# Two tiles of an output projection stand beside other heads of the attention in a two-layer SSD, retention and attention step

## The reference, cut to what matters

```python
u = h @ lp['w_in']
y_ssd, ssd_state = _ssd(...)        # 8 heads x 64
y_ret, ret_state = _retention(...)  # 4 heads x 64
y_mla, ckv, krope = _mla(...)       # 4 heads x 64, softmax attention
mix = jnp.concatenate([y_ssd, y_ret, y_mla], axis=-1)   # width 1024
x = x + g1 * (mix @ lp['w_out'])
h2 = _rmsnorm(x, lp['norm2_w']) * (1 + sc2) + sh2
a, gt = jnp.split(h2 @ lp['ffn_w1'], 2, axis=-1)
x = x + g2 * ((jax.nn.silu(a) * gt) @ lp['ffn_w2'])
```

## Time and profile before

| what | value |
|---|---|
| median of 3 runs | 1047.66 us (1045.16 to 1050.39) |
| the profiled execution's own time | 1046.3 us |
| its span | 1043.4 us |
| PE busy | 1017.8 us (98%) |
| DVE busy | 632.6 us (61%) |
| ACT busy | 439.5 us (42%) |
| mean granted clock of PE | 0.997 |

### The profile page before, as it was taken

How to read it: one execution, slowest core, us unless ns; L and a number is a source line. 1 busy time by engine, 2 the same in 40 slices (tenths; PEclk the granted TensorE clock), 3 DMA queues, 4 the chain that set the end, 5 groups by cost and what they waited for, 6 DMA issues and landing times.

```text
span 1043.4 us, 16435 instructions
## 1 busy us (share of the span) xinstructions
PE 1017.8 (98%) x6552; PEld 931.5 (89%) x6552; DVE 632.6 (61%) x1134; ACT 439.5 (42%) x684; POOL 105.3 (10%) x99
## 2 busy tenths in 40 slices
PE   7899999999999999999999999999999999999995
PEld 4698996779999989999999899667999999999995
DVE  6686868868555543534448786887765555444333
ACT  3256445456333332343334755735543333323221
POOL 0004323003000000000101233400300000000100
PEclk9999999999999999999999999999999999999998
DMA  9843245314333478333464224451243333723431
GB/s 382 335 165 128 82 161 202 130 64 149 139 132 128 161 291 325 112 113 114 136 244 161 92 84 150 165 216 41 90 153 121 121 121 121 278 89 111 132 117 60
DMA packets 30678, 159.56 MB, mean 153 GB/s; under 512 B 3424, under 2 KB 4384, under 8 KB 19872
## 3 DMA queue, kind: packets, MB, share of 16 engines
q1 hardware_dynamic: 28896, 146.75, 38.9%
q10 hardware_dynamic: 1728, 12.06, 2.8%
HBM read 156.27 MB, written 2.52 MB: 152 GB/s over the span
## 4 chain that ended last, share of the span: by engine, by line
PE 92%; DVE 4%; ACT 2%; ACTq 1%; issue 1%; DMA 1%; POOL 0%; DVEq 0%; POOLq 0%
PE ps L476 26%; PE ps L478 26%; PE ps L477 25%; PE ps L505 3%; DVE wlo L1356 1%; PE ps L803 1%; PE ps L720 1%; PE ps L922 1%; PE ps L747 1%; PE ps L572 1%; PE ps L901 1%; ACTq L1068 1%; PE ps L824 1%; ACT whi L1018 1%; DMA adas<-wada_dram 1%
## 5 line engine op out<-in xcount | busy, mean ns | idle before, releaser
L476 PE MATMUL ps<-h_hi,whi 128*128 128x386 f32 (+1 forms) x1120 | 384.7, 344 | 0.6 <-issue 0.5
L478 PE MATMUL ps<-h_hi,wlo 128*128 128x386 f32 (+1 forms) x1120 | 379.7, 339 | 0.0
L477 PE MATMUL ps<-h_lo,whi 128*128 128x386 f32 (+1 forms) x1120 | 378.7, 338 | 0.0
L1356 DVE TENSOR_TENSOR wlo<-stage,whi 128x2048 fp32r<-128x2048 f32 (+1 forms) x106 | 223.3, 2107 | 154.2 <-ACT whi L1018 154.2
L1018 ACT ACTIVATE whi<-stage 128x2048 fp32r<-128x2048 f32 (+1 forms) x106 | 185.9, 1754 | 229.1 <-PE ps L478 210.7
L476 PEld LDWEIGHTS ps<-h_hi,whi 128*128 128x128 f32 x1120 | 211.3, 189 | 9.5 <-issue 7.0
L477 PEld LDWEIGHTS ps<-h_lo,whi 128*128 128x128 f32 x1120 | 211.6, 189 | 0.3
L478 PEld LDWEIGHTS ps<-h_hi,wlo 128*128 128x128 f32 x1120 | 210.6, 188 | 0.0
L476 PE MATMUL ps<-hid_hi,whi 128*128 128x384 f32 x352 | 118.3, 336 | 0.0
L478 PE MATMUL ps<-hid_hi,wlo 128*128 128x384 f32 x352 | 118.3, 336 | 0.0
L477 PE MATMUL ps<-hid_lo,whi 128*128 128x384 f32 x352 | 118.3, 336 | 0.0
(11 more groups left out here) (295 smaller groups left out, 1131.1 us busy)
## 6 DMA issues: line engine op xcount, KB each, us to landing
stage<-wf_dram SPq DMA_DIRECT2D x44, 1024.0 KB, 4.8
adas<-wada_dram SPq DMA_DIRECT2D x80, 512.0 KB, 5.7
stage<-wf_dram SPq DMA_DIRECT2D x32, 704.0 KB, 4.1
stage<-win_dram SPq DMA_DIRECT2D x20, 1024.0 KB, 4.8
stage<-wout_dram SPq DMA_DIRECT2D x8, 1024.0 KB, 5.6
adaf<-wada_dram ACTq DMA_DIRECT2D x6, 1024.0 KB, 15.2
small<-small_dram SPq DMA_DIRECT2D x2, 1202.5 KB, 8.7
stage<-win_dram ACTq DMA_DIRECT2D x2, 1024.0 KB, 13.3
```

Of the source, the lines that this page charges most:

```text
L476: mm(out, ah, bh, start=(k == 0), stop=False)
L477: mm(out, ah, bl, start=False, stop=False)
L478: return mm(out, al, bh, start=False, stop=(k == n - 1))
L1356: tt(wlo[:, g % 2, 0:width], stage[:, g % 2, 0:width], whi[:, g % 2, 0:width].bitcast(F32), ALU.subtract)\
```

## The change

The list of the heads beside which the eight first-half tiles stand has 3 in place of 4 and 7 in place of 8. Tile 2 thus stands in step 3 of PE, tile 5 in step 7; DVE's residual of tile 2 stands in step 4, that of tile 5 in step 8 (ahead of the split of block 13 in that step). Tiles 0, 1, 3, 4, 6 and 7 keep their steps.

```diff
-BESIDE_HEADS = (1, 2, 4, 5, 6, 8, 9, 11)
+BESIDE_HEADS = (1, 2, 3, 5, 6, 7, 9, 11)
```

## The result

| | median of the runs | against before, ratio (95% interval) |
|---|---|---|
| before | 1047.01 us (12 runs) | |
| changed | 1053.65 us (12 runs, 1051.82 to 1058.15) | 1.0066 (1.0054 to 1.0077) |

The change makes the kernel slower by 6.6 us. The forecast was 4.2 us more (1051.9); the time lies in its range (1048.0 to 1055.5), but above the 0.5% within which the forecast saw its likeliest case.

What follows compares the result with a forecast made beforehand. PE was taken to bound the kernel (92% of the chain), taking turns with DVE in the attention. 2.41 - 0.33 = 2.08 us a layer, 4.2 for two, on 1047.66 gave 1051.9 us; range 1048.0 to 1055.5.

Steps and rivals of the forecast that it cites:

- likeliest case: Attention of both layers: the PE and DVE ping-pong is stretched ahead of the weight split, +2.0 to +5.2 us, 1051.9; chance 0.66.
- The replay of the order: Attention, PE and DVE timelines of layer 0 reworked with tiles 2 and 5 moved: 2.08 us a layer, 4.2 for two.
- transposes 8 start: PE, attention: delayed 2.41 us to 220.88, PE's wait of 0.67 there becoming about 2.7 us.
- the attention at full clock: Each layer's attention: 2.41 late at transpose 8 less 0.33 given back, 2.08 us longer.
- The residual of tile 2 now stands ahead of maximum 5: DVE, attention: this residual costs 0.55, so with the 0.90 of maximum 4, maximum 5 is late by 1.45 us.
- Behind a wait it takes 0.13 more: PE, transposes of head 4: 0.55 for three against 0.42 without a wait, putting scores of head 7 1.06 us late.
- Nothing in it absorbs a delay: DVE and ACT chain around the weight split, maximum 8 to transpose 8: the 2.41 us delay passes on whole.
- The give-back: Transpose 9 on PE: residual of tile 5 no longer behind normalisation 8, so a 0.28 wait and 0.05 restart go, 0.33.
- by the rows, it stayed at 1.00 through 2 us without a matmul, and the sum leaves it out: PE clock in the new wait of about 2.7 us: taken as staying at 2.4 GHz, no time added.
- rival (c): New wait before transpose 8: clock falls, work to tile 7's end takes twice as long, +4.8 a layer, +13.8, 1061.5; chance 0.03.
- or if the clock row shows under 1.00 in the attention: Sign against the prediction: granted clock in the attention was to read 1.00 in the changed profile.
- Rival (d): Not slower: tiles fill PE's waits before transposes 2 and 6, -1.2 us, 1046.5, if maximum 8 late leaves transpose 8 unaffected; chance 0.09.

Runs made afterwards that it cites:

- early split: ACT's high half of weight block 13 written in step 5, not 8: changed kernel 1047.21 us, 0.9997 of before; kernel before 1045.71 us, 0.9984.
- second run: The changed kernel itself timed and profiled once more, nothing further changed: 1054.85 us median, 1.0065 of before.
- the run with the filled wait: The changed kernel plus 14 matmuls of unused result per layer in PE's wait before the transposes of head 8: 1051.92 us, 1.0043 of before.

## Why the prediction was right, and where it fell short

**The replay of the order held.** Its times, and those of the changed kernel less the 0.15 of its later start:

| step of the prediction | forecast | measured |
|---|---|---|
| tile 2 starts | 197.95 | 197.95 |
| maximum 4 starts | 201.01 | 201.02 |
| transposes 4 start | 206.05 | 206.03 |
| scores of head 7 start | 209.18 | 209.09 |
| scores of head 8 start | 212.37 | 212.20 |
| transposes 8 start | 220.88 | 220.72 |
| PE's wait there | about 2.7 | 2.62 |
| the attention at full clock | +2.08 | +2.01 |

"The residual of tile 2 now stands ahead of maximum 5", at 0.55, was right: maximum 5 came at 204.71, and 203.27 + 1.45 is 204.72. "Behind a wait it takes 0.13 more" was half wrong: from transposes 4 to the products behind them it took 0.48 (206.18 to 206.66), so 0.06 more, and tile 5 follows its transposes by 0.24 (209.89 to 210.13) where 0.33 was taken; so everything from head 7 on came 0.1 to 0.2 earlier than forecast. "Nothing in it absorbs a delay" held: maximum 8 was 2.24 late and transposes 8 were 2.25 late. The runs with the early split show what could have absorbed some of it: there DVE doesn't wait for ACT in that chain, and 2.25 at maximum 8 become 1.24 at transposes 8. The give-back behind them can be read in layer 1, at full clock: transposes 8 were 2.25 late (26.88 us behind the first scores before, 29.13 now) and the attention 2.01 longer, so 0.24 was given back where the prediction had 2.41 and 0.33.

**The step that failed is the clock.** The prediction weighed it and then wrote "by the rows, it stayed at 1.00 through 2 us without a matmul, and the sum leaves it out", and gave rival (c) 0.03. By its own last sentence, "or if the clock row shows under 1.00 in the attention", it was wrong here, though the time came out in its range. But the earlier trace rows show one instance, at the end of the kernel, where no matmul follows: the last one ended at 1033.27 and the clock fell only in the stretch from 1036. That told little of a wait in the midst of the work. In the profiled executions with a wait of 2.6 us there are six such attentions, and the clock fell in five; in the four with the wait filled and the eight with no wait of transposes over 0.8 us it fell in none. The Trainium skill (TensorE: Matmul & The Clock Gate, "Why this matters for your kernels") warns of a clock that falls back to half when TensorE idles between bursts of matmuls. The trace agrees with the mechanism, but the page speaks of longer gaps than the 2.62 us that were followed by a fall here, and here the measurement decides.

Rival (c) had the right mechanism and the wrong price, 4.8 us a layer. It let all work up to the end of tile 7 run at half clock. Measured against the same order at full clock, a fall took 1.6 (changed kernel, layer 0), 1.6 and 3.0 (second run), 1.6 and 2.8 us (tile 5 alone): in the changed kernel's layer 0 it fell 1.1 us behind the wait and was back before 226, while tile 7 ran. The stretches give the same price: (1 - 0.50) x 2 + (1 - 0.64) x 2 = 1.7 us. The two dear falls, 3.0 and 2.8, are the two that began within the wait. Even they cost less than 4.8: tile 7 ended at full clock, and at half clock its matmuls came every 0.32 us against 0.18, less than twice.

**The sum as measured.** The order is worth 1.0043 - 1 = 0.43% (4.5 us) in the run with the filled wait, or 4.0 us by the two attentions. The clock is the rest of 0.65%: some 0.2%, 2.3 us an execution (2.9 by the medians). The two intervals overlap by a little, so that size is rough. The forecast, 0.40%, was the order; 0.32 for a slowdown above 0.5% was low because that third of the loss was priced at nothing.

**Rival (d)**, not slower, fell at the point named for it: maximum 8 was late and transposes 8 were late with it. It would have fallen without the dependence on exponential 8 as well: with the early split in both kernels the change still made the attention 1.4 us longer.

**Left open:** what decides whether and when the clock falls at a given wait. The same wait, to 0.01 us, was followed by a fall in layer 0 and not in layer 1 of one execution; of the five falls two began within the wait and three 1.1 to 1.3 us behind it. Nor was it tried whether fewer filling matmuls do, or what makes up the 1.4 us a layer that the change costs with the early split.

## What to carry to other kernels

Where two engines take turns, work put into a place where one waits may stand in front of what the other waits for next: look at what is queued behind that, here a weight split of 4 us, before counting the wait as room. To price a change together with a second one, run the second one in both kernels: the early split alone looked as if it took back all but 0.2 of the 2.0 us, but 1.2 of that it gives the kernel before too. A wait of TensorE like the one of 2.6 us here is to be priced with its clock as well, as a range (here 0 to 3.0 us), and every place of its kind is to be read for it, since one showed a fall and the next none. The instruction worth moving was not a matmul but the copy on ACT, which had been placed behind an exponential that it didn't need.

## What the runs showed that was not expected

- Adding 14 useless matmuls of 0.18 us in each layer made the kernel 2.9 us faster in the median (1054.85 to 1051.92, same chip and rounds; the intervals overlap by a little), by keeping TensorE's clock at 2.4 GHz in the attention.
- The clock also falls in the first 40 us, whatever was changed: it did in the profiles of six of the seven experiments (not in that of the early split in the kernel before), and in neither of the two first profiles, of before and of the changed kernel. There too a wait of PE stands ahead of it, for DVE at L583, and it is shorter: 1.5 to 1.7 us. Of the eight profiles with that wait six show the fall, beginning 0.3 to 1.7 us behind it; in the ninth, the one of the early split in the kernel before, the wait is 0.99 and the clock stays. So waits well under 2.6 us can be followed by a fall. No run filled this one. In the profile of tile 2 alone the stretches 0 to 20 and 20 to 40 us had 0.97 and 0.94, and its attention began at 193.16 in place of 191.59. That scatter, about 1.5 us, has nothing to do with the two tiles.

```profile
...
17.71 0.61 PE L583 MATMUL ps<-const,adac 128*128 128x2 f32 x4 [1.70 <-DVE adac L1455]
...
```

```profile
0.00:20.00 20.00, 14.65 (x60) 7.63 (x64) 10.89 (x16) 7.54 (x11) 0.20 (x4) 0.97 0.91 370
20.00:40.00 20.00, 17.67 (x144) 10.99 (x140) 14.36 (x38) 4.43 (x6) 0.00 (x0) 0.94 0.86 355
```
